# Final norm of a hybrid encoder trunk: residual squares one expert block earlier, norms ahead of the last sums, one closing wait moved from GpSimd to SP

## What is computed

```python
def rms_norm(x, w):
    xf = x.astype(jnp.float32)
    y = xf * lax.rsqrt(jnp.mean(xf * xf, axis=-1, keepdims=True) + EPS)
    return (y * w.astype(jnp.float32)).astype(x.dtype)

def expert_choice_ffn(h, w_router, w_gate, w_up, w_down):
    ...
    cap = CAPACITY_FACTOR * n_tok // N_EXPERTS
    probs = jax.nn.softmax(t.astype(jnp.float32) @ w_router.astype(jnp.float32), axis=-1)
    aff, idx = lax.top_k(probs.T, cap)
    xe = t[idx]
    hid = jax.nn.silu(jnp.einsum("ecd,edf->ecf", xe, w_gate)) * jnp.einsum("ecd,edf->ecf", xe, w_up)
    ye = jnp.einsum("ecf,efd->ecd", hid, w_down) * aff[..., None].astype(h.dtype)
    out = jnp.zeros_like(t).at[idx.reshape(-1)].add(ye.reshape(-1, d))
    return out.reshape(bsz, seq, d)

    ...
    x = x + expert_choice_ffn(rms_norm(x, norm_ffn_w), w_router, w_gate, w_up, w_down)
    ...
    return rms_norm(x, norm_final_w)
```

## Time and profile before

| | |
|---|---|
| Time, median of 3 executions | 2436.92 us (2433.25 to 2437.91) |
| Profiled execution, time | 2433.38 us |
| Profiled execution, span | 2431.2 us, mean granted clock 0.993 |
| TensorE matmul busy | 98% of the span |
| VectorE, ScalarE, GpSimd busy | 44%, 21%, 13% |
| DMA: moved over the span | 707.01 MB, mean 291 GB/s |
| Chain that ended last, by engine | PE 94%, DVE 3%, issue 1%, DMA 1%, ACT 1% |

### The profile page before, as it was taken

The page is one execution under the profiler, slowest core; times in us unless marked ns, Lnnn a source line. Parts: engine busy times, 40 slices in busy tenths (PEclk is TensorE's granted clock), DMA queues, the critical chain, the costliest instruction groups (busy, mean ns, idle before and its releaser), DMA issues.

```text
span 2431.2 us, 49823 instructions
## 1 busy us (share of the span) xinstructions
PE 2388.9 (98%) x22095; PEld 1659.8 (68%) x22095; DVE 1074.4 (44%) x2029; ACT 514.4 (21%) x1059; POOL 305.4 (13%) x418
## 2 busy tenths in 40 slices
PE   9899999999999999999999999999999999999996
PEld 9788998899898888845655555555555555555553
DVE  6989889888987634322221221222122122212213
ACT  5445444444533512100000000000000000000001
POOL 0313332441341000000000000000000000000001
PEclk9899999999999999999999999999999999999998
DMA  5133333233235545699999999999999999999996
GB/s 185 56 126 98 98 102 128 88 100 126 98 127 203 211 145 207 239 367 415 410 420 409 416 410 419 414 409 420 409 418 410 419 414 409 419 410 414 416 410 239
DMA packets 88488, 707.01 MB, mean 291 GB/s; under 512 B 11633, under 2 KB 15857, under 8 KB 51409
## 3 DMA queue, kind: packets, MB, share of 16 engines
q1 hardware_dynamic: 65360, 628.93, 63.7%
q0 software_dynamic: 14272, 56.60, 7.5%
q10 hardware_dynamic: 8640, 18.29, 2.0%
HBM read 669.72 MB, written 34.06 MB: 289 GB/s over the span
## 4 chain that ended last, share of the span: by engine, by line
PE 94%; DVE 3%; issue 1%; DMA 1%; ACT 1%; POOL 0%; ACTq 0%; POOLq 0%; DVEq 0%
PE p_gu L2467 38%; PE pp L1150 18%; PE p_y L2485 10%; PE p_y L2488 6%; PE pp L1358 6%; PE pp L1194 5%; PE pp L1391 2%; PE p_z L2488 2%; PE pdg L1245 2%; PE off_banks L1228 1%; PE ptr L1212 1%; PE pp L1480 1%; PE off_banks L1242 1%; PE off_banks L1240 1%; DVE room L1597 0%
## 5 line engine op out<-in xcount | busy, mean ns | idle before, releaser
L2467 PE MATMUL p_gu<-raw,xT 128*32 128x512 f32 (+1 forms) x8304 | 932.2, 557 | 0.8 <-ACT xT L2345 0.8
L2467 PEld LDWEIGHTS p_gu<-raw,xT 128*32 128x32 f32 x8304 | 420.9, 110 | 348.6 <-issue 155.4
L2363 DVE SCALAR_TENSOR_TENSOR tg<-tg,p_gu 128x256 f32<-128x256 f32 (+1 forms) x144 | 57.4, 398 | 1068.8 <-ACT tg L2327 1064.4
L2485 PE MATMUL p_y<-raw,hidT 128*32 128x384 f32 x3744 | 433.3, 487 | 0.0
L1150 PE MATMUL pp<-h,wx_hi 128*128 128x256 f32 (+1 forms) x1664 | 424.0, 346 | 0.5 <-ACT fo L736 0.5
L2327 ACT ACTIVATE tg<-p_gu 128x256 f32<-128x256 f32 (+1 forms) x144 | 52.7, 366 | 1266.0 <-PE p_gu L2467 1266.0
L2488 PE MATMUL p_y<-raw,hidT 128*32 128x256 f32 x1248 | 320.3, 379 | 0.0
L1150 PEld LDWEIGHTS pp<-h,wx_hi 128*128 128x128 f32 x1664 | 282.9, 190 | 31.2 <-ACT fo L736 0.7
L1150 PE MATMUL pp<-h,wx_lo 128*128 128x256 f32 (+1 forms) x832 | 281.4, 338 | 0.0
L2488 PEld LDWEIGHTS p_y<-raw,hidT 128*32 128x32 f32 x1248 | 137.3, 110 | 129.8 <-issue 48.8
L2488 PE MATMUL p_z<-raw,hidT 128*32 128x256 f32 x624 | 185.6, 379 | 0.0
(11 more groups left out here) (271 smaller groups left out, 2928.4 us busy)
## 6 DMA issues: line engine op xcount, KB each, us to landing
raw<-in_w_e SPq DMA_DIRECT2D x185, 2048.0 KB, 24.7
raw<-in_w_e SPq DMA_DIRECT2D x58, 1536.0 KB, 23.6
raw_first<-in_w_e SPq DMA_DIRECT2D x23, 2048.0 KB, 24.8
w_raw<-in_w_x SPq DMA_DIRECT2D x48, 512.0 KB, 3.5
dec<-acs POOLq DMA_DIRECT2D x48, 512.0 KB, 4.8
raw<-in_w_e SPq DMA_DIRECT2D x16, 1024.0 KB, 25.6
w_raw<-in_w_g SPq DMA_DIRECT2D x24, 512.0 KB, 3.5
g_tab<-gx POOLq DMA_DIRECT2D x8, 1152.0 KB, 5.8
```

What stands on the lines that cost most here:

```text
L2363: dve.scalar_tensor_tensor(out=tg[:, r % 2, 0:w], in0=tg[:, r % 2, 0:w], scalar=1.0, in1=p[:, 0:w], op0=ALU.add, op1=ALU.mult).then_inc(s_ ...
L2467: mm = pe.matmul(p_gu[g][quad(q), 0:w], xT[:, e % 2, k * SLOTS + 32 * g:k * SLOTS + 32 * (g + 1)], slot[:, at:at + w], start=(k == 0), sto ...
L2485: pe.matmul(y_first[half][quad(g), :], hidden(g), w[:, half * 3 * P:(half + 1) * 3 * P], start=first, stop=last)
```

## The change

`SQUARES_AT` becomes 140, the last round of the block before the last, so that ScalarE's six squares stand ahead of the tanhs of rounds 141 to 143. Three norms stand behind round 140 on VectorE, the other three behind round 143, ahead of the sums. The wait for the indirect stores (`f_put`) goes from GpSimd to SP, behind its wait for the plain stores. Nothing is computed differently, and no instruction is added or taken away.

```diff
--- before.py
+++ after.py
@@ -2205,9 +2205,8 @@
         y_last = [t[quad(3), 0:2 * P] for t in (p_y[:, 0:512], p_y[:, 512:1024], p_z)]
         LAST_AT = 6 * P
 
-        SQUARES_AT = ROUNDS - 1
-        NORMS_AT = ROUNDS - 1
-        FIRST_NORMS = 3
+        SQUARES_AT = ROUNDS - 1 - GROUPS
+        NORMS_AT = {ROUNDS - 1 - GROUPS: range(0, NT // 2), ROUNDS - 1: range(NT // 2, NT)}
 
         def listed(engine):
 
@@ -2248,6 +2247,7 @@
                 sp.wait_ge(f_o, t + 1)
                 sp.dma_start(out[0, row:row + P, :], of[t]).then_inc(f_out, 16)
             sp.wait_ge(f_out, 16 * NT)
+            sp.wait_ge(f_put, 32)
 
         @block.gpsimd
         def _(pool):
@@ -2314,7 +2314,6 @@
                 pool.indirect_dma_start(out.rearrange("b s d -> (b s) d"),
                                         bass.IndirectOffsetOnAxis(ap=ids[0:hi - lo, 0:1], axis=0),
                                         xg[lo:hi, :], None).then_inc(f_put, 16)
-            pool.wait_ge(f_put, 32)
 
         @block.scalar
         def _(act):
@@ -2424,13 +2423,10 @@
                     if r == tokens_at(e):
                         for g in range(GROUPS):
                             tokens(e, g)
-                if r == NORMS_AT:
-                    for t in range(FIRST_NORMS):
-                        norm(t)
+                for t in NORMS_AT.get(r, ()):
+                    norm(t)
             summed(0)
             summed(1)
-            for t in range(FIRST_NORMS, NT):
-                norm(t)
             for b in range(2):
                 dve.wait_ge(f_rs, 2 * NT + 2)
                 cols = slice(b * 512, (b + 1) * 512)
```

## The result

| | before | changed |
|---|---|---|
| Time, median of 8 executions | 2436.52 us (2433.25 to 2439.39) | 2443.58 us (2439.47 to 2447.57) |
| Ratio, 95% interval | | 1.0031 (1.0022 to 1.0041) |
| Profiled execution, span | 2431.2 us | 2437.3 us |

The change makes the kernel 0.31% slower. The profiled execution of the changed kernel is the fastest of its eight, as that of the kernel before was near the fast end of its own; the two spans differ by 6.1 us, the medians by 7.1.

What follows compares the result with a forecast made beforehand. TensorE's matmuls were taken to bound the kernel, other engines only behind the last matmul. 9.5 + 1.4 - 1.95 - 0.99 - 2.0 = +6.0 us on the median 2436.92 gave 2442.9 us, range 2437.0 to 2448.5.

Steps and rivals of the forecast that it cites:

- the likeliest case: Slower by over 0.2%, that is above 2441.8 us, given 0.68; same 0.25, faster 0.07.
- the stall: TensorE before the last block's output matmuls: idle while the tanh of round 141 waits for squares, +9.5 us (8.0 to 11.0).
- the clock: Output matmuls behind TensorE's gap: 2.82 us of them at half clock, +1.4 us (bounds 0 and +7.8).
- GpSimd's scale without norms beside it: Behind the last matmul: GpSimd's two instructions on the gathered rows take 0.86 us instead of 2.81, -1.95 us.
- No wait for the plain stores: Behind the last matmul: GpSimd no longer waits for the normed tiles' stores before the indirect stores, -0.99 us.
- GpSimd's DRAIN ahead of the landing: Program end: DRAIN starts right behind the second indirect store's issue and keeps its 4.73 us, -2.0 us.
- VectorE's three norms ahead would cost nothing: Before the last hidden values: norms end before the tanh does, costing 0; if late, each adds 1.28 us.
- The three gains: Behind the last matmul: GpSimd's undisturbed scale -1.95, no wait for normed tiles' stores -0.99, earlier DRAIN -2.0 us.
- the DRAIN's end hangs on the stores' landing: Rival at the program's end: the 2.0 us are not gained, +8.0 us in all, 2444.9 us; chance 25%.
- The half clock through all six steps: Rival in the output matmuls: clock stays at 0.50, they take 15.6 us, 2449.3 us in all; chance 7%.
- the tiles would be there in time: Rival at the squares: residual tiles land early enough, no stall remains, -4.9 us, 2432.0 us; chance 13%.

Runs made afterwards that it cites:

- three squares: Changed kernel with all six norms behind round 143, only squares 0 to 2 ahead of the tanhs and 3 to 5 behind round 143: 2439.82 us, ratio 1.0014.
- last three experiments: Kernel before with only the wait on SP, 2433.18 us; changed kernel with squares and norms behind round 143, 2436.02; the latter with norm weights read from PSUM, 2431.93.

## Why the prediction was right

It gave 2442.9 us and the likeliest case by its mechanism; measured were 2443.58. The mechanism held step by step. That on the profiled executions the sum of 6.0 us met 6.1 so closely is luck: two terms, the stall and the clock, were off by 1.5 and 1.6 us in opposite ways. On the medians the difference was 7.1.

| Step of the prediction | forecast | measured in the changed kernel |
|---|---|---|
| Tanh of round 141 behind the squares, TensorE's stall | +9.5 | +8.0 |
| Half clock in the output steps | +1.4 | +3.0 |
| GpSimd's scale without norms beside it | -1.95 | -1.96 |
| No wait for the plain stores | -0.99 | -1.01 |
| GpSimd's DRAIN ahead of the landing | -2.0 | -2.2 |
| Start of the tail, no part of the change | 0 | +0.3 |

**The stall** was the mechanism as stated. From the tanh of round 140 to the first output matmul it is 2412.04 - 2375.85 = 36.2 us against 2403.74 - 2375.51 = 28.2 before. The 1.5 us too many are mostly two: the sixth tile landed 31.5 us behind that tanh instead of 32.5, and VectorE's three rounds took 2411.97 - 2408.73 = 3.2 us, the sum of their instructions, and not 3.5. That VectorE's three norms ahead would cost nothing came true with little to spare: slowed by GpSimd's scales they followed each other every 2.0 us, which the prediction did not reckon with, and the third ended 0.3 us before the hidden values could begin. One row was read loosely: in the kernel before the sixth square waited for its tile, but the first, at 2401.70, stood behind ScalarE's last tanh and not behind its tile, which had landed at 2401.2.

**The clock** is the term that was mis-sized. From the first output matmul to the first sum it is 2422.56 - 2412.04 = 10.5 us against 2411.28 - 2403.74 = 7.5. The forecast took the length of the half clock from one gap of the kernel before (2.82 us of matmuls, rows 9). That kernel has another, which the forecast left out: TensorE is idle for 5.4 us before 94.37, and the clock is back only at 106.7 (windows of TensorE before):

```profile
94.37:99.70 5.33, 3.96 (x15) 0.50 0.46 157
102.40:106.70 4.30, 4.30 (x13) 0.50 0.00 0
```

There 8.3 us of matmuls, with pauses between them, ran at half clock. The runs with a gap here show 6.0 us (changed), 2.9 (all norms behind round 143), 5.6 (three squares) and 5.9 (loads on ScalarE's queue): the row was the low end and not the middle. The measured 3.0 lay inside the bounds given.

**The three gains** behind the last matmul came as worked out: 2427.51 - 2422.56 = 4.95 us from the first sum to VectorE's last pair against 2418.19 - 2411.28 = 6.91; then 2429.90 - 2428.92 = 0.98 us to the first indirect store against 1.99 (2421.59 - 2419.60); and 7.4 us from there to the end against 9.6.

**The rivals.** That the DRAIN's end hangs on the stores' landing, and that moving the wait gains nothing, falls with the run that moved the wait alone. Some 4.7 us come again in every kernel, which speaks for a fixed cost and against the wait that this rival took the DRAIN for; this is argued, not shown. The half clock through all six steps did not come; the changed kernel had it for 6.0 of the 10.9 us that they took. That the tiles would be there in time falls: in the eight profiled executions with the loads on SP's queue the sixth landed 30.8 to 32.5 us behind the start of the tanh of round 140, and the first tanh that it can hold up was started by the kernel before 2398.77 - 2375.51 = 23.3 us behind it.

What the medians show beyond the profile: the changed kernel's eight executions go from 2439.47 us at a mean granted clock of 0.993 to 2447.57 at 0.989. Within that list a longer time never goes with a higher clock; the executions of the kernel before beside the last three experiments go the same way (2433.79 us at 0.993 to 2442.11 at 0.990). Whether the longer ones have the half clock for longer in the tail or elsewhere is open, since only the fastest was profiled.

## What to carry to other kernels

Moving an instruction up in an engine's order does not move it up in time when its data come late; it puts the data's arrival in front of everything behind it on that engine, here the three tanhs that TensorE needed. Before moving such work ahead, read when its load lands, not when it is issued, and price the idle time of TensorE with the slow matmuls that follow it. And price the parts of an edit apart: two of the three here were gains, worth 5.1 us of tail (4.3 on the medians) once the third was left out and the norms no longer slowed GpSimd.

## What the runs showed of the hardware that was not expected

GpSimd's DRAIN at the end of the program is long, and it can be run beside the landing of the stores. In the kernel before it started behind the landing and took 4.73 us; in the other kernels, all with the wait on SP, it started within the first store's issue and ended 4.6 to 4.7 us behind the end of the second's. A second DMA queue brought the first of six loads 12 us sooner and the last 3.7 us later. And the length of a gap did not set how long the half clock lasted behind it: gaps of 4.9, 7.8, 8.2 and 11.1 us left TensorE 5.6, 6.0, 2.9 and 5.9 us of matmuls at 1.2 GHz. What did set it no run shows.
